# Three chunk pairs of a projection by Strassen's scheme, in a two-layer decoder step on one core

## Time and profile before

| | |
|---|---|
| median of 3 runs | 963.71 us (958.22 to 967.72) |
| profiled execution | 962.66 us, span 961.0 us |
| PE busy | 908.9 us, 95% of the span |
| DVE, ACT, POOL busy | 478.8, 293.4 and 249.8 us |
| mean granted clock of PE | 0.988 |
| DMA read and written | 108.70 and 11.36 MB |
| chain that ended last | PE 82%, DVE 5%, ACT 3%, DMA 2%, POOL 2% |

### The profile page before, as it was taken

How to read it: one execution, slowest core, us unless ns; L and a number is a source line. 1 busy time by engine, 2 the same in 40 slices (tenths; PEclk the granted TensorE clock), 3 DMA queues, 4 the chain that set the end, 5 groups by cost and what they waited for, 6 DMA issues and landing times.

```text
span 961.0 us, 15871 instructions
## 1 busy us (share of the span) xinstructions
PE 908.9 (95%) x5210; PEld 482.1 (50%) x5210; DVE 478.8 (50%) x965; ACT 293.4 (31%) x716; POOL 249.8 (26%) x353
## 2 busy tenths in 40 slices
PE   6999999999899999999999999999799998887998
PEld 3544444444455553444565676566544444444444
DVE  1156777778545553122224253724677776766211
ACT  5101111013354542023101010423655565664100
POOL 0000232310023440240434242000443344357000
PEclk9999999999999999999999999999899998998999
DMA  9142665594144547793234142130122133033211
GB/s 352 57 176 93 230 219 177 206 296 95 45 133 132 176 141 262 287 211 102 74 103 137 39 137 67 41 90 12 38 63 67 51 99 105 1 92 108 91 45 45
DMA packets 82487, 117.61 MB, mean 122 GB/s; under 512 B 21006, under 2 KB 45790, under 8 KB 82094
## 3 DMA queue, kind: packets, MB, share of 16 engines
q1 hardware_dynamic: 61824, 78.87, 24.8%
q0 software_dynamic: 10944, 29.41, 10.4%
q10 hardware_dynamic: 9648, 8.41, 2.7%
HBM read 108.70 MB, written 11.36 MB: 125 GB/s over the span
## 4 chain that ended last, share of the span: by engine, by line
PE 82%; DVE 5%; issue 3%; ACT 3%; DMA 2%; POOL 2%; POOLq 1%; SPq 0%; ACTq 0%; DVEq 0%
PE ps L729 26%; PE ps L986 11%; PE ps L992 6%; PE ps L1290 6%; PE ps L738 4%; PE ps L1048 3%; PE ps L1009 3%; PE ps L924 3%; PE ps L902 2%; PE ps L1171 2%; PE ps L1160 2%; DMA arena<-cache_sb_v 2%; PE ps L874 2%; DVE work L1997 2%; PE ps L1026 1%
## 5 line engine op out<-in xcount | busy, mean ns | idle before, releaser
L729 PE MATMUL ps<-wring,arena 128*128 128x512 f32 x448 | 198.4, 602 | 1.5 <-issue 1.5
L729 PEld LDWEIGHTS ps<-wring,arena 128*128 128x128 f32 x448 | 85.1, 192 | 105.8 <-issue 105.7
L668 POOL TENSOR_TENSOR z<-z,work 128x1024 f32<-128x1024 f32 (+1 forms) x64 | 80.2, 1254 | 157.1 <-DVE work L2005 156.7
L986 PE MATMUL ps<-wring,z 128*128 128x512 f32 (+2 forms) x320 | 106.7, 488 | 0.0
L1522 ACT ACTIVATE z<-ps,work 128x512 f32<-128x512 f32 (+3 forms) x128 | 66.4, 525 | 73.5 <-DVE work L1997 70.6
L1345 ACT ACTIVATE z<-ps 128x512 f32<-128x512 f32 (+1 forms) x64 | 27.4, 433 | 181.8 <-PE ps L729 147.5
L360 POOL DMA_DIRECT2D arena<-cache_sb_k x64 | 34.5, 539 | 164.7 <-DVE work L1640 141.2
L986 PEld LDWEIGHTS ps<-wring,z 128*128 128x128 f32 x320 | 54.8, 190 | 43.4 <-issue 41.8
L1845 DVE TENSOR_TENSOR arena<-ps,consts 128x512 f32<-128x512 f32 x32 | 30.3, 1020 | 82.3 <-PE ps L1026 82.3
L1802 DVE TENSOR_TENSOR xres<-xres,ps 128x512 f32<-128x512 f32 (+1 forms) x32 | 15.5, 484 | 86.4 <-PE ps L1290 38.9
L1997 DVE TENSOR_REDUCE work<-ps 128x1 f32<-128x512 f32 (+3 forms) x128 | 56.9, 486 | 2.2
(11 more groups left out here) (320 smaller groups left out, 1264.4 us busy)
## 6 DMA issues: line engine op xcount, KB each, us to landing
wring<-w_in SPq DMA_DIRECT2D x12, 2048.0 KB, 9.2
arena<-cache_sb_k POOLq DMA_DIRECT2D x64, 256.0 KB, 3.0
arena<-cache_sb_v SPq DMA_DIRECT2D x64, 256.0 KB, 3.5
wring<-w_out SPq DMA_DIRECT2D x3, 2048.0 KB, 8.2
arena<-cache_sel_k SPq DMA_DIRECT2D x64, 64.0 KB, 1.8
consts<-aux SPq DMA_DIRECT2D x1, 2315.5 KB, 15.5
xres<-x_prompt SPq DMA_DIRECT2D x4, 512.0 KB, 9.3
wring<-w_in SPq DMA_DIRECT2D x2, 1024.0 KB, 8.4
```

Of the source, the lines that this page charges most:

```text
L668: nc.gpsimd.tensor_tensor(P_u(n), P_u(n), bc(coef(n).unsqueeze(2), [P, 2, (NT - n % NT) * P]), ALU.mult).then_inc(n_scaled, 1)
L729: mm = pe.matmul(ps[:, t, 0:width], stat, mov, start=(k == 0), stop=(k == KT - 1))
L986: mm = pe.matmul(ps[:, bank, at:at + w], normed1(k, t), wring[:, slot, k, lo:lo + w], start=(k == 0), stop=(k == KT - 1))
```

## The change

Six sections become three pairs, (SQ, SK), (RQ, RK) and (RV, RG). A pair is one matrix product of 512 tokens by 1,024 by 1,024, cut into two by two blocks, of tokens, of model columns and of output columns (one section each). Strassen's scheme, in the variant of Winograd, needs 7 block products instead of 8, and sums of blocks before and after:

- the input sums S1 to S4 (256 tokens by 512 columns each), once, by DVE;
- four weight sums for each pair, by POOL: `t3_sum`, and three written in place over the weight blocks once the sample rows have used these;
- the output sums: on DVE (`pair_sums`, from PSUM) and on POOL (`output_sums`).

A weight block is a quarter of `wring` (128 by 2,048 values, 1 MB); a pair fills all four. The gate section SG is done plainly between the first and second pair, from weights loaded into unused parts of `z`; the value section SV is plain too and stands last. The rotation of RQ goes from DVE to POOL (`rotate_q`). Page products take two pages at a time. SP issues the key page loads, between the quarter loads. Seven small products are put ahead of the first input turn. Output stores of keys and values move to the end of the projection. In layer 1 `cmp_scale` goes ahead of `load_values`.

```diff
+SQ, SK, SG, RQ, RK, RV, RG, SV = range(8)
+SECTION = [4, 5, 7, 0, 1, 2, 3, 6]
...
+        pool_sum, POOL_PAIR, POOL_SUMS = n_scaled, [0, 8, 16], 25
+        dve_sum, DVE_PAIR, DVE_SUMS = n_c, [1, 7, 13], 19
+        MM_IN0 = 3 * 16 + 2 * 5
...
+        def xpart(name, k, t):
+
+            if name in xsum:
+                return xsum[name][:, k, t * P:(t + 1) * P]
+            row, half = {"A11": (0, 0), "A12": (0, 1), "A22": (2, 1)}[name]
+            return xnT[:, half * (KT // 2) + k, (row + t) * P:(row + t + 1) * P]
...
+                def keys(first, last):
+
+                    load_pages(sp, "cache_sb_k", page_loaded, 0, first, last)
+
+                keys(0, 1)
+                sp.wait_ge(mm_done, MM_PAIR[0] + 14)
+                for q, section, half in ((3, RK, 1), (2, RK, 0)):
+                    quarter_load(q, section, half)
+                sp.wait_ge(mm_done, MM_PAIR[0] + 16)
+                for half in range(2):
+                    quarter_load(half, RQ, half)
+                keys(1, 8)
+                sp.wait_ge(mm_done, MM_PAIR[1] + 8)
+                sp.wait_ge(pool_sum, POOL_PAIR[1] + 3)
+                quarter_load(3, RV, 0)
+                keys(8, 10)
+                sp.wait_ge(mm_done, MM_PAIR[1] + 12)
+                quarter_load(2, RG, 1)
+                sp.wait_ge(mm_done, MM_PAIR[1] + 14)
+                sp.wait_ge(pool_sum, POOL_PAIR[1] + 4)
+                quarter_load(0, RG, 0)
+                keys(10, 11)
+                sp.wait_ge(mm_done, MM_PAIR[1] + 16)
+                quarter_load(1, RV, 1)
+                keys(11, NB * NPG // 4)
+                sp.wait_ge(mm_done, MM_PAIR[2] + 8)
+                sp.wait_ge(pool_sum, POOL_PAIR[2] + 4)
+                quarter_load(2, SV, 0)
                 sp.wait_ge(ds_scores, 1)
                 for u in range(2):
                     sp.dma_start(by_pair(A_rs)[halves(u)], ins["state_ret"].rearrange("b (a u) d e -> u d b a e", u=2)[u]).then_inc(rs_in, 16)
...
                 load_pages(sp, "cache_sb_v", vpage_loaded, NB * NPG, 0, 1)
-                sp.wait_ge(bank_free, 5 + 5 * 7)
...
+                def weight_sums(p, step):
+
+                    b11, b21, b12, b22 = QUARTERS[p]
+                    loads = [(1, 1, 1, 1), (2, 2, 2, 2), (3, 3, 3, 3)][p]
+                    if step == 0:
+                        pool.wait_ge(q_loaded[b22], 16 * loads[b22])
+                        pool.wait_ge(q_loaded[b12], 16 * loads[b12])
+                        pool.wait_ge(mm_done, MM_PAIR[p - 1] + 10) if p else None
+                        nc.gpsimd.tensor_tensor(t3_sum, quarter(b22), quarter(b12), ALU.subtract).then_inc(pool_sum, 1)
+                    else:
+                        n0 = POOL_PAIR[p] + (2 if p == 2 else 1)
+                        pool.wait_ge(mm_done, MM_PAIR[p] + 6)
+                        pool.wait_ge(q_loaded[b11], 16 * loads[b11])
+                        pool.wait_ge(pool_sum, n0)
+                        nc.gpsimd.tensor_tensor(quarter(b12), quarter(b12), quarter(b11), ALU.subtract).then_inc(pool_sum, 1)
+                        pool.wait_ge(pool_sum, n0 + 1)
+                        nc.gpsimd.tensor_tensor(quarter(b11), quarter(b22), quarter(b12), ALU.subtract).then_inc(pool_sum, 1)
+                        pool.wait_ge(q_loaded[b21], 16 * loads[b21])
+                        pool.wait_ge(pool_sum, n0 + 2)
+                        nc.gpsimd.tensor_tensor(quarter(b21), quarter(b21), quarter(b11), ALU.subtract).then_inc(pool_sum, 1)
+
+                def output_sums(p):
+
+                    sA, sB = PAIRS[p]
+                    n0 = POOL_PAIR[p] + (5 if p == 2 else 4)
+                    for t in range(2):
+                        pool.wait_ge(bank_free, FREE_PAIR[p] + 9 + t)
+                        nc.gpsimd.tensor_tensor(v_sum(t), sec(2 + t, sA), sec(t, sB), ALU.subtract).then_inc(pool_sum, 1)
+                    for t in range(2):
+                        pool.wait_ge(dve_sum, DVE_PAIR[p] + 5 + t)
+                        pool.wait_ge(pool_sum, n0 + 2)
+                        nc.gpsimd.tensor_tensor(sec(2 + t, sB), sec(t, sB), v_sum(t), ALU.add).then_inc(pool_sum, 1)
+
+                def rotate_q():
+
+                    hf = DH // 2
+                    pool.wait_ge(pool_sum, POOL_PAIR[2] + 1)
+                    pool.wait_ge(dve_sum, DVE_PAIR[1] + 6)
+                    pool.wait_ge(bank_free, FREE_PAIR[1] + 10)
+                    for t in range(NT + 1):
+                        r = rows[t]
+                        x = heads(sec(t, RQ))
+                        cos = bc(cst("cosine", r)[:, t * DH:(t + 1) * DH].unsqueeze(1), [r, H, DH])
+                        sin = cst("sine", r)[:, t * DH:(t + 1) * DH]
+                        a, b = v_sum(0)[0:r], v_sum(1)[0:r]
+                        st.done(nc.gpsimd.tensor_tensor(heads(a), x, cos, ALU.mult))
+                        st.done(nc.gpsimd.tensor_tensor(heads(b)[:, :, 0:hf], x[:, :, hf:DH], bc(sin[:, 0:hf].unsqueeze(1), [r, H, hf]), ALU.mult))
+                        st.done(nc.gpsimd.tensor_tensor(heads(b)[:, :, hf:DH], x[:, :, 0:hf], bc(sin[:, hf:DH].unsqueeze(1), [r, H, hf]), ALU.mult))
+                        add = nc.gpsimd.tensor_tensor(sec(t, RQ), a, b, ALU.add)
+                        st.done(add) if t < NT else add.then_inc(pool_sum, 1)
+
+                for p in range(3):
+                    weight_sums(p, 0)
+                    if p == 2:
+                        rotate_q()
...
+                    weight_sums(p, 1)
+                    output_sums(p)
...
+                        cmp_scale(n // 8)
                     if n in (32, 33):
...
-                    if n % 8 == 2:
-                        cmp_scale(n // 8)
...
+                def product(bank, x, w, t, onto=False):
+
+                    for k in range(KT // 2):
+                        mm = pe.matmul(ps[:, bank, :], xpart(x, k, t), w[:, k], start=(k == 0 and not onto), stop=(k == KT // 2 - 1),
+                                       skip_group_check=True)
+                    mm.then_inc(mm_done, 1)
...
+                        elif p == 1:
+                            pe.wait_ge(bank_free, free - 5 + t + 1)
+                        else:
+                            pe.wait_ge(bank_free, FREE_PAIR[1] + 3 + t)
...
+                    else:
+                        pe.wait_ge(dve_sum, before + 3)
+                    plain_rows(4, from_quarters(b11, b21))
+                    pe.wait_ge(dve_sum, before + 1) if p else None
...
+                    pe.wait_ge(q_loaded[b22], loads)
+                    plain_rows(5, from_quarters(b12, b22))
...
+                        product(6 + t, "S3", t3_sum, t)
+                    if between:
+                        between()
+                    pe.wait_ge(pool_sum, sums + 2)
+                    for t in range(2):
+                        pe.wait_ge(bank_free, free + 7 + t)
+                        product(2 + t, "S1", quarter(b12), t, onto=True)
+                    pe.wait_ge(pool_sum, sums + 3)
+                    for t in range(2):
+                        pe.wait_ge(bank_free, free + (6, 5)[t])
+                        product((5, 4)[t], "S2", quarter(b11), t)
+                    pe.wait_ge(pool_sum, sums + 4)
+                    for t in range(2):
+                        pe.wait_ge(bank_free, free + 9 + t)
+                        product(6 + t, "A22", quarter(b21), t, onto=True)
+
+                pe.wait_ge(zeroed_stats, 2)
+                for _ in range(7):
+                    pe.matmul(ps[:, 7, 0:2 * P], S_ret[:, 0, :], flat(S_ret[:])[:, 0:2 * P], start=True, stop=True)
                 pe.wait_ge(s_first, 16)
-                turn_x(0, 0)
-                pe.wait_ge(w_first, 16)
+                pair(0)
+                pe.wait_ge(xr_loaded, 32)
                 for t in range(NT):
-                    project_tile(0, 0, t, xnT_ready, 0,
-                                 halfway=(second_half, lambda: turn_x(0, 2), lambda: turn_x(0, 3), lambda: turn_x(0, 4))[t])
-                project_rows(0, 0, xnT_ready, 0)
...
-                    pe.wait_ge(w_loaded[n % 2], 16 * (n // 2 + 1))
-                    project(n, n % 2, xnT_ready, 0, turned_out=(n == SG))
+                    pe.wait_ge(bank_free, FREE_PAIR[0] + 4) if t == 0 else None
+                    pe.wait_ge(dve_sum, DVE_PAIR[0] + 2 * (t - 2) + 2) if t >= 2 else None
+                    plain_tile(SG, t, t, from_sections, turned_out=True)
+                plain_rows(4, from_sections)
+                pair(1)
...
                                   start=(j % NPG < 4), stop=(j % NPG >= 4)).then_inc(page_free, 1)

-                pe.wait_ge(w_loaded[RG % 2], 16 * (RG // 2 + 1))
+                pair(2)
+                pe.wait_ge(bank_free, FREE_PAIR[2] + 4)
...
+                dve.wait_ge(xn_ready, NT)
+                st.done(TT(xsum["S1"], half[2], half[3], ALU.add))
+                st.done(TT(xsum["S2"], xsum["S1"], half[0], ALU.subtract))
```

(31 more changed lines are left out.)

330 lines of the change are left out of this document (216 added, 114 removed).

## The result

Changed kernel: 1000.44 us (median; 997.33 to 1001.39), kernel before on the same chip: 965.04. The ratio of the times is 1.037, with a 95% interval of 1.033 to 1.041: slower, by 35 us. The forecast was 981, its range ended at 992. The profiled execution after spans 998.8 us against 961.0, 37.8 more. Where a time in a trace is compared with one before, both count from the start of the span.

A forecast was written before the change was run, and what follows sets the result against it. The prediction took PE to bound the projection before the change, with some room on DVE. With the branch loop 23 us later and 5 saved afterwards, 962.66 + 23 - 5 = 980.7, said as 981; range 950 to 992.

The forecast's parts named there:

- The walk up to pair 2's end: Projection: pair 0 ends at 74.4 us, page products start at 103.7, first in-place sum at 226.6, pair 2 ends at 250.3.
- rival 4: Key page loads on SP come late, one us in each of 11 rounds: kernel 992 us; chance 0.10.
- POOL's chain: Pair 1's output sums, `t3_sum`, `rotate_q`, first in-place sum of pair 2: 32.4 us, plus 10 for DVE's products.
- The value section: Last section before the branch loop: turn, SV and rows, scores, small turns and sums take 33.8 us, ending at 284.
- Afterwards: Behind the branch loop's start: 0 us for stores ahead of value page loads, -5 (0 to -8) for layer 1.
- both waits should go: Layer 1: two products' waits of 1.70 and 3.20 us for `cmp_scale` behind page loads vanish: -5 us (0 to -8).
- PE's first steps cover a load of that length: Branch loop: stores ahead of the first value page loads cost 0 to 3 us, taken as 0.
- say 30 us: Projection: all DVE and POOL waits at the shared port, 4.4 + 5 + 10 + 10, and 2 in the last normalisation.
- rival 1: Half the port's waits miss each other: loop starts near 270, kernel 966 us; chance 0.18.
- rival 2: No price at the port: loop starts at 255, kernel 951 us, the late rotation costing PE some 13; chance 0.17.
- The chance of a gain, 0.21: Chance of the kernel being faster by more than about 1%, 9.6 us: rivals 2 and 3 together.
- Rival 3: PE stays the bound, weight sums all in time and pair 2 unhindered: kernel 935 us; chance 0.04.

The follow-up runs named there:

- rotate_later: Changed kernel with `rotate_q` on POOL moved from ahead of pair 2's three in-place weight sums to behind them: 1000.45 us, ratio 1.040.
- no_port: Changed kernel with page products, input sums and normalising products on DVE replaced by reductions with one SBUF operand: 971.53 us, ratio 1.009.
- one_input: Changed kernel with each page product replaced by a reduction with one SBUF operand, leaving out the multiplication by the query: 981.87 us, ratio 1.017.
- swap_undone: Changed kernel with layer 1's `cmp_scale` put back behind the two `load_values`: 998.06 us, ratio 1.037.
- short_sums: Changed kernel with eleven of POOL's twelve weight sums cut to an eighth of their columns: 979.2 us, ratio 1.017.
- turn_later2: rotate_later with two value tiles ahead of the first turn, small turns behind the third, second value quarter issued before the state loads: 995.69 us, ratio 1.032.
- no_port_turn: turn_later2 with the same DVE instructions replaced by one-operand reductions as in no_port: 959.75 us, ratio 0.997.
- warmup_alone: Kernel before with only the seven warm-up products of PE added ahead of the first weights: 961.8 us, ratio 0.9986.

## Why the prediction was right and wrong

**The walk up to pair 2's end was right, in part by luck.** Forecast and measured: pair 0's end 74.4 and 75.0; page products from 103.7 and 104.9; POOL's first in-place sum ready at 226.6 and 227.4; pair 2's end 250.3 and 251.1. DVE's sums of pair 1 ended 4.8 us late, at 188.6: the key pages of rounds 8 and 10 (counted from 0, as in the prediction) came 3.0 and 3.3 us late behind weight quarters, a part of rival 4. POOL's chain behind them made that good: it took 38.7 us, where the prediction has 32.4 + 10. The two misses cancel, and so 227.4 says less for the walk than it seems to. (The prediction's own terms add up to 226.2, not 226.6.)

**The value section was sized 2.4 us short**, 33.8 for 36.15 (252.90 to 289.05, with 1.8 us of issue ahead of the loop's first sums), behind a wait of 1.8 for SK's normalisation where I had the two chains level. With pair 2's 0.8 that makes PE's 284 into 289: a loop 27 us late, not 23. The mechanism held.

**The step that failed is "Afterwards".** I put it at 0 for the stores ahead of the value pages and at -5 (0 to -8) for layer 1; in the trace it is +10.6 (709.7 against 699.1), and this is most of what the forecast missed.
- Layer 1: "both waits should go". They did go, 4.9 us in sum (a third, of 2.7 us, stayed). What I did not ask is what the exchange puts `load_values` behind: the value pages are issued after `cmp_scale`, and PE waits 6 us for them. The exchange alone costs 2.4 to 3.6 us, so the term was wrong by some 8 and in sign. For POOL's work in the projection I had named who is queued behind what; here I had not.
- The value pages of the loop: "PE's first steps cover a load of that length". One wait of 5.2 us says no; the granted clock is at 0.5 from 298.0 to 304.8 after it, and the loop lasts 2.45 us longer, which goes with the 2.6 us of waits that the change adds. Moving the stores moved the wait, so the stores alone are not shown to be the cause.
- What is left of the 10.6, some 3 to 5 us, stays open. In the changed kernel 2.8 us arise just ahead of layer 1's first scores, where the clock is at 0.5 in three stretches between 690 and 714; `rotate_later`, the same code there, has one such stretch and does not lose them, but loses 2.4 near 483. It goes with the low clock, and where that falls differs from kernel to kernel; its cause was not tried.
- The sign does not hang on one trace: the rest is 702.7 to 711.3 us in the ten kernels here that keep all that the change does behind the loop's start, and 697.4 to 699.6 in the three that have none of it. The size does: 10.6 is near the upper end.

**The port.** Mechanism and direction were right, and the size was near: I put all waits there at "say 30 us", and DVE's chain ends 29.4 us earlier without it. That the two agree so closely is luck, since 10 of my 30 are delays of POOL by DVE's products, and the 29.4 is DVE's. It speaks against rival 1, half the price, all the same. The page "SBUF — State Buffer" of the Trainium skill, section "Who interferes with whom", gave the same rule for DVE instructions on two SBUF operands, and the products with one operand bear it out. But rival 2, no price, was worked out wrong: I let the loop start at 255 and the kernel take 951, and `no_port`, which is that case, starts it at 264.40 and takes 971.53, 8.5 us more than the kernel before. That rival counted the late rotation, and left out the weight quarters behind the key pages (8.7 us there), which my walk through pair 2 names for a POOL that is fast. About half of the 20.5 us between 951 and 971.53 lies behind the loop's start (a rest of 704.5), where that sum has the forecast's -5. The chance of a gain, 0.21, rested mostly on that sum. Rival 1's 966 lies between the two sums and shares these errors; how much too low it is, no run shows. Rival 3, PE stays the bound, is ruled out by the waits of the changed kernel.

## What to carry to other kernels

When work is taken off the busiest engine and given to two others that share a port, price the port first: here DVE was at 66%, and 29 us of waits at the end of its chain were more than the 20.7 us that PE saved. A long wait that disappears without moving the end (15.5 us for POOL, replaced by 19.2 for DVE) means that chains are level: look for the next one before repairing the first. And when two instructions are exchanged in an in-order queue, one of them goes later: name who waits for the one that now goes second, and what that costs, before the gain of the other is booked.

## What the runs showed of the hardware

- POOL's sum of 2,048 columns takes 4.49 to 4.53 us alone, the 2.1 ns a column of the earlier trace rows, so that the slope holds over a factor of eight (0.72 for 256).
- A DVE instruction with one SBUF operand waits for POOL as well, where it is a TENSOR_SCALAR: the same one on 512 columns took 3.07 us beside POOL's sum, 2.11 in `one_input` beside another, and 0.43 in the kernel before (below), less than the 0.69 of an instruction on two operands. A TENSOR_REDUCE never did: 1.22 us each, alone or beside POOL. The section of the Trainium skill named above has both: it counts `tensor_scalar` among the operations that can take the shared port pair, and says that `tensor_reduce` cannot on this chip. The runs agree.

```profile
210.30 0.43 DVE L1643 TENSOR_SCALAR work<-work 128x512 f32<-128x512 f32 x1 [0.22 <-DVE work L1642]
```

- Warm-up products worked in eight of the fourteen traces that have them: the first 8 passes take 3.67 to 3.70 us in place of 6.72 (in the changed kernel after 6.3 us of products in the idle start). In the other six (`one_input`, `swap_undone`, `short_sums`, `turn_later2`, `no_port`, `no_port_turn`) they take 5.3 to 6.7, and the granted clock is at 0.5 for 3.4 or 6.8 us from 9 to 12 us on. What decides between the two was not tried. In the trace of `warmup_alone` the products are worth 3.6 us, and its median shows no difference.
